# Routing interleaved with the output projection by token tile, expert weights loaded in pieces

## The chip, the core and the metric

The kernel runs on one core of a Trainium2 chip. TensorE (PE) multiplies matrices, VectorE (DVE) and ScalarE (ACT) do elementwise work and read PSUM, GpSimd (POOL) does elementwise work and issues the indirect transfers, SyncE (SP) issues most DMAs, and 16 DMA engines move the data. The metric is the device time of one execution in microseconds (us).

## The reference

Two layers (`DEPTH = 2`) over 512 tokens (`SEQ`) of width 1024 in float32, then a final RMSNorm:

```
for l in range(DEPTH):
    h = rms_norm(x, attn_norm_g[l]);  proj = h @ w_in[l]
    ya = banded_attention(...) @ w_branch_a[l]      # 8 heads, sinks
    yb = dilated_attention(...) @ w_branch_b[l]     # 3 groups of 4 heads
    merged = sigmoid(gate_a) * ya + sigmoid(gate_b) * yb
    x = x + merged @ w_out[l]                       # output projection
    x = x + hier_moe(rms_norm(x, ffn_norm_g[l]), ...)
```

`hier_moe` computes 4 group logits and 32 expert logits for each token, takes the best group, the best two experts inside it, and adds the two experts' SwiGLU outputs (1024 to 2 x 256 to 1024), weighted.

## The kernel before

A token tile is 128 tokens; there are four (`TT`), t = 0 to 3. Each layer goes through these stages.

- Projections, attention and gates, to about 372 us in the first layer. Weight tiles of 512 KB are streamed through a ring of two buffers (`raw`) by SP (`load_tile`); ACT rounds a tile to `w_hi` (`split_hi`, line 779), DVE computes the rest `w_lo` (`split_lo`, line 980), and TensorE makes three products (`three`, lines 431 to 433: hi*hi, lo*hi, hi*lo). `w_hi`/`w_lo` also have two buffers. SP may load tile i when tile i-2 has been split. Two semaphores carry this: `hi_ok`, `lo_ok` (a tile is split), and `w_used` (TensorE has used it).
- Output projection: eight weight tiles, called here out tiles 0 to 7. The loop `for dh in range(2)` goes over the two halves of the output columns, inside it `for kp in range(4)` over the weight tiles, and inside that over the four token tiles. Columns 0 to 511 of token tile t gather in bank t, columns 512 to 1023 in bank 4+t. DVE adds the banks to `x` (`xo_ok`). While this goes on, SP loads the weights of expert pair 0 and then of pair 1 in pieces of 512 KB (`load_piece`), between the `raw` tiles, all in one queue.
- Routing, after the last out tile: squares of `x` on ACT, `rstd` on DVE, transposes of `x` on TensorE (line 647) and copies into `xtr`, router logits (line 615), a second transpose, the normalised rows `xn2` (`h2_tile`) stored to DRAM by POOL (`h2_rows`, line 1392), and then on DVE a long chain of small instructions from the logits (line 1173) to the assignment `asg` (line 1212). TensorE adds up the assignments (`bank[6]`), DVE turns them into ranks (`rankm`), selections (`sel`, `choose`) and, with a matmul (`read_info`, line 669), into row indices (`slots`: `idx_h`, `idx_y`). `keep_busy` (line 447) are matmuls whose result nobody reads.
- Experts: 16 pairs. For pair n: POOL gathers its rows (`gather`, line 1397), TensorE turns them (`rows_in`, line 675), `up` (line 681) multiplies with the weights `gu`, then SiLU, `turn_z`, and `down` (line 694) with `dn`; POOL scatters the rows. The weights are 4 MB (`gu`) and 2 MB (`dn`) a pair in a ring of three buffers (`RING`). Pair 2's weights lie on the merged activations and may be loaded only when the output projection has ended (`w_used`); pair p's may be loaded when pair p-3 is done with its buffer (`gu_ok`, `dn_ok`).
- At the layer's end SP loads the scattered rows (`yld`) and DVE adds them to `x`.

Of the kernel before, what the change touches and what calls it, by code (L numbers as in the profile page):

```python
# [9 lines left out]
I32 = mybir.dt.int32  # L10
# [22 lines left out]
MORE_AT = {s: sum(1 for n in range(2, PAIRS) if n % RING == s) for s in range(RING)}  # L33
# [56 lines left out]
K_ORDER = [6, 7, 0, 1, 2, 3, 4, 5]  # L90

# [7 lines left out]
def hybrid_encoder(nc, x_in, stream, gu_w, dn_w, params, g_rows, consts, masks, out):  # L99
# [27 lines left out]
    info = at("info", o, [TT, 2, NE], F32R); o = after(o + 4 * TT * 2 * NE)  # L127
    idx_y = at("idx_y", o, [PAIRS], I32); o = after(o + 4 * PAIRS)
    idx_h = at("idx_h", o, [PAIRS], I32); o = after(o + 4 * PAIRS)
    small = at("small", o, [288], FP32); o = after(o + 4 * 288)  # L130
    gl8 = small[:, 96:128].rearrange("p (t n) -> p t n", n=8)
    cum = small[:, 128:288].rearrange("p (t n) -> p t n", n=NE)
# [30 lines left out]
    w_hi = [at(f"w_hi{i}", R_S + (8 + 8 * i) * KB, [1024], F32R) for i in range(2)]  # L163
    w_lo = [at(f"w_lo{i}", R_S + (12 + 8 * i) * KB, [1024], F32R) for i in range(2)]
    xtr = at("xtr", R_S + 8 * KB, [KD, T], FP32)
# [4 lines left out]
    xn2 = [at(f"xn2_{t}", R_H + 48 * KB + 4 * KB * t, [D], FP32) for t in range(2)] + [at("xn2_2", R_S, [D], FP32)]  # L170
# [4 lines left out]
    junk = at("junk", R_S + 4 * KB, [2, D], BF16)  # L175
    sel = at("sel", R_S + 4 * KB, [2, TT, P], F32R)

    rt = at("rt", R_S + 16 * KB, [2048], FP32)
# [20 lines left out]
    rankm = word(TT * NE, TT, NE)  # L199
    wts = word(TT * 8, TT, 8)  # L200
    elog = word(TT * NE, TT, NE)
    lgt = word(T)
    lsc = word(TT * NLOG, TT, NLOG)
    top_g = word(TT * 8, TT, 8)
    idx_g = word(TT * 8, TT, 8)
    top_e = word(TT * 8, TT, 8)
    idx_e = word(TT * 8, TT, 8)
    idxf = word(TT * 3, TT, 3)
    oh_g = word(TT * NGRP, TT, NGRP)
    el8 = word(TT * 8, TT, 8)  # L210
    oh1 = word(TT * NE, TT, NGRP, EPG)
    oh2 = word(TT * NE, TT, NGRP, EPG)
    elm = oh1
    oh8 = word(TT * 2 * EPG, TT, 2, EPG)
    asg = word(TT * NE, TT, NE)
    rtmp = elog
    ge = word(TT * NGRP, TT, NGRP)
    assert _w[0] <= 2048, _w[0]
# [9 lines left out]
    spare = small[:, 64:65]  # L228

    ctx = ExitStack()  # L230
    with ctx:
# [31 lines left out]
        h2_ok, h2_st0, h2_st = sems("h2_ok", "h2_st0", "h2_st")  # L263
# [58 lines left out]
        def _(sp):  # L322
# [46 lines left out]
            with sp.Fori(0, L) as l:  # L369
# [17 lines left out]
                for p in range(2, PAIRS):  # L387
                    if p >= RING:
                        sp.wait_ge(gu_ok, l * PAIRS + p - RING + 1)
                    load_gu(l, p)  # L390
                    if p >= RING:
                        sp.wait_ge(dn_ok, l * PAIRS + p - RING + 1)
# [1135 lines left out]
```

## Time and profile before

| | us |
|---|---|
| three runs | 1416.78, 1419.51, 1419.99 (median 1419.51) |
| the profiled execution's own time | 1414.65 |
| its span | 1413.0 |
| TensorE busy | 1241.5 (88%) |
| VectorE busy | 592.0 (42%) |
| ScalarE busy | 398.2 (28%) |
| GpSimd busy | 240.0 (17%) |
| mean granted TensorE clock | 0.955 of full speed |

The span is the time from the first to the last instruction in the profile. A busy TensorE is not one at its peak. Each time in the rows below is counted from the span's start; a releaser in square brackets names what the engine had waited for before the row.

### The profile page before, as it was taken

The page shows a single profiled execution, that of the slowest core. Times are in us where ns is not written, and L with a number is a line of the kernel's source. Part 1 is how long each engine was busy: PE and PEld are TensorE (multiplying, and loading weights), DVE is VectorE, ACT ScalarE, POOL GpSimd, SP SyncE. Part 2 cuts the span into 40 slices and gives each one's busy share as a digit, 9 for nine tenths or more (in the row PEclk, how much of TensorE's full clock was granted, in tenths as well). Part 3 has the DMA queues.
Part 4 walks back from the last instruction along what each step waited for, and adds up shares of the span by engine and source line. Part 5 has one row for each costly group of instructions (what it writes and reads, how often), then busy time and mean ns, then how long its engine had stood idle before and what let it go on. Part 6 is the DMA issues. An engine that isn't in the chain of part 4 may idle for free.

```text
span 1413.0 us, 18694 instructions
## 1 busy us (share of the span) xinstructions
PE 1241.5 (88%) x6416; PEld 813.5 (58%) x6417; DVE 592.0 (42%) x1395; ACT 398.2 (28%) x731; POOL 240.0 (17%) x183
## 2 busy tenths in 40 slices
PE   5999988999997998887489999889999979978881
PEld 5877766788884433332177777667888734423330
DVE  4467676233344222221254677753333432322115
ACT  5334335333231110000153444444332300100003
POOL 0314140022101111111003233201220011111100
PEclk9999999999999999998899999999999989999996
DMA  5432220463544899999433222106437539999975
GB/s 185 127 96 84 76 90 2 149 218 108 205 183 186 367 424 424 424 424 417 162 122 116 90 91 90 45 16 223 164 104 283 217 123 424 423 423 425 424 333 199
DMA packets 59486, 306.76 MB, mean 217 GB/s; under 512 B 11376, under 2 KB 11376, under 8 KB 45056
## 3 DMA queue, kind: packets, MB, share of 16 engines
q1 hardware_dynamic: 48256, 281.57, 51.3%
q0 software_dynamic: 10992, 23.25, 4.4%
q8 instruction: 50, 0.82, 0.2%
q10 hardware_dynamic: 144, 0.76, 0.1%
q14 instruction: 44, 0.36, 0.1%
HBM read 290.33 MB, written 23.07 MB: 222 GB/s over the span
## 4 chain that ended last, share of the span: by engine, by line
PE 61%; DMA 21%; DVE 7%; issue 4%; ACT 3%; DVEq 3%; SPq 0%; ACTq 0%; POOL 0%; POOLq 0%
DMA gu<-in_gu_w 17%; PE bank L431 13%; PE bank L433 13%; PE bank L432 13%; PE bank L681 10%; PE bank L694 4%; PE bank L566 2%; DVEq L1062 1%; DMA h_rows<-xn 1%; ACT prob L850 1%; PE bank L502 1%; DVE prob L1085 1%; PE bank L675 1%; PE bank L533 1%; DMA yld<-y_rows 1%
## 5 line engine op out<-in xcount | busy, mean ns | idle before, releaser
L681 PE MATMUL bank<-gu,xgt 128*64 128x512 f32 x1024 | 245.9, 636 | 49.8 <-DMA gu<-in_gu_w 46.8
L431 PE MATMUL bank<-h_hi,w_hi 128*128 128x512 f32 x640 | 253.4, 396 | 6.1 <-DVE h_lo L1022 3.6
L433 PE MATMUL bank<-h_hi,w_lo 128*128 128x512 f32 x640 | 249.5, 390 | 0.0
L432 PE MATMUL bank<-h_lo,w_hi 128*128 128x512 f32 x640 | 249.1, 389 | 0.0
L980 DVE TENSOR_TENSOR w_lo<-raw,w_hi 128x1024 fp32r<-128x1024 f32 x112 | 139.2, 1243 | 185.2 <-ACT w_hi L779 184.3
L681 PEld LDWEIGHTS bank<-gu,xgt 128*64 128x64 f32 x1024 | 79.1, 146 | 213.1 <-issue 168.5
L779 ACT ACTIVATE w_hi<-raw 128x1024 fp32r<-128x1024 f32 x112 | 118.1, 1055 | 101.2 <-PE bank L433 101.2
L431 PEld LDWEIGHTS bank<-h_hi,w_hi 128*128 128x128 f32 x640 | 120.2, 188 | 32.4 <-DVE h_lo L1022 4.0
L433 PEld LDWEIGHTS bank<-h_hi,w_lo 128*128 128x128 f32 x640 | 120.1, 188 | 25.5
L432 PEld LDWEIGHTS bank<-h_lo,w_hi 128*128 128x128 f32 x640 | 120.3, 188 | 23.7
L694 PE MATMUL bank<-dn,zt 128*64 128x512 f32 x512 | 116.9, 598 | 6.2 <-ACT zt L939 3.3
L1294 DVE TENSOR_TENSOR z<-bank,sil 128x256 f32<-128x256 f32 x32 | 13.6, 425 | 248.2 <-ACT sil L937 248.2
L1369 POOL TENSOR_TENSOR swp<-swp,cst 128x512 f32<-128x512 f32 x34 | 48.7, 1431 | 289.2 <-DMA swp<-pj 289.2
L937 ACT ACTIVATE sil<-bank 128x256 f32<-128x256 f32 x32 | 12.3, 384 | 293.7 <-PE bank L681 293.7
L1397 POOL DMA_INDIRECT xg<-h_rows,idx_h x32 | 32.4, 1012 | 350.8 <-DVE idx_y L1254 337.3
L850 ACT ACTIVATE prob<-prob,small 128x256 f32<-128x256 f32 (+2 forms) x96 | 64.7, 675 | 58.4 <-DVE small L1067 58.4
L1384 POOL TENSOR_TENSOR mab<-mab 128x512 f32<-128x512 f32 x16 | 35.2, 2199 | 263.8 <-DVE mab L1135 263.8
L1085 DVE TENSOR_SCALAR prob<-prob,small 128x256 f32<-128x256 f32 (+2 forms) x96 | 73.5, 807 | 5.1 <-issue 1.7
L694 PEld LDWEIGHTS bank<-dn,zt 128*64 128x64 f32 x512 | 34.0, 136 | 64.6 <-issue 55.3
L1268 DVE COPY yb<-bank 128x512 f32<-128x512 f32 x32 | 22.1, 692 | 110.4 <-PE bank L694 63.1
L933 ACT ACTIVATE yb<-bank 128x512 f32<-128x512 f32 x32 | 19.1, 597 | 134.5 <-PE bank L694 76.2
L1033 DVE TENSOR_TENSOR rca<-pj,cst 128x512 f32<-128x512 f32 x34 | 29.7, 872 | 50.1 <-ACT pj L837 50.1
(181 smaller groups left out, 1627.2 us busy)
## 6 DMA issues: line engine op xcount, KB each, us to landing
gu<-in_gu_w SPq DMA_DIRECT2D x28, 4096.0 KB, 37.6
raw<-in_stream SPq DMA_DIRECT2D x112, 512.0 KB, 3.4
dn<-in_dn_w SPq DMA_DIRECT2D x28, 2048.0 KB, 36.6
gu<-in_gu_w SPq DMA_DIRECT2D x32, 512.0 KB, 5.5
swp<-pj SPq DMA_DIRECT2D x136, 64.0 KB, 2.0
dn<-in_dn_w SPq DMA_DIRECT2D x16, 512.0 KB, 5.7
yld<-y_rows SPq DMA_DIRECT2D x16, 512.0 KB, 7.1
h_rows<-xn POOLq DMA_DIRECT2D x8, 512.0 KB, 10.5
```

What stands on the lines that cost most here:

```text
L431: mm(dst, ah, bh, start=start, stop=False)
L432: mm(dst, ah, bl, start=False, stop=False)
L433: return mm(dst, al, bh, start=False, stop=stop)
L681: last = mm(bank[b][e * CAP:(e + 1) * CAP, :], xgt[:, x_s, k, e * CAP:(e + 1) * CAP], gu[w_s][:, e, k, :], start=k == 0, stop=k == KD - 1)
L694: last = mm(bank[4 + half][e * CAP:(e + 1) * CAP, :], zt[:, f, e * CAP:(e + 1) * CAP], dn[w_s][:, e, f, half * T:(half + 1) * T], start=f ...
L779: run(w_hi[i % 2][:, :], raw[:, i % 2, :], ACT.Copy).then_inc(hi_ok, 1)
L850: last = run(p, p, ACT.Exp, bias=nmx[:, 2 * s + h:2 * s + h + 1], scale=-1.0, accum_out=rsum[:, 2 * s + h:2 * s + h + 1])
L980: tt(w_lo[i % 2][:, :], raw[:, i % 2, :], w_hi[i % 2][:, :].bitcast(FP32), ALU.subtract).then_inc(lo_ok, 1)
L1085: last = ts(p, p, den[:, 2 * s + h:2 * s + h + 1], None, ALU.mult)
L1369: g.tensor_tensor(swp[:, r % 2, :], swp[:, r % 2, :], c(C_SIN, T), ALU.mult).then_inc(sn_ok, 1)
L1384: g.tensor_tensor(mab[:, half, 0, :], mab[:, half, 0, :], mab[:, half, 1, :], ALU.add).then_inc(sum_ok, 1)
L1397: pool.indirect_dma_start(out=xg[n % 2][:, :], out_offset=None, in_=h2_rows[:, :], in_offset=bass.IndirectOffsetOnAxis(ap=idx_h[:, n:n + 1 ...
```

## The change

It has four parts. (1) The second half of the output projection goes over token tiles outside and weight tiles inside; between them stand the transposes of `x` (`turn_x`) and the router logits, each in half tiles (`HALVES`). The logits are computed with the tokens on the partitions, so the second transpose goes. For this all four weight tiles of the second half must be held at once: `OUT_SLOT` gives them two more buffers. (2) The routing on DVE is done in two groups of two token tiles (`choose_group`, `rank_group`): the first inside the projection, the second after it. `h2_tile` and the transposes' copies are on ACT; the count of rounds and the weights `wts` come after the first three `slots`. (3) The weights of pairs 2, 3, 13, 14 and 15 are loaded in pieces (`PARTS`), `dn` in two, and `up_pair` waits for each piece. (4) Pair 2's `gu` is split around the first two gathers: SP waits for them before its last two pieces; pair 3's first piece waits for the first half of pair 0's `up` (`gu_half`).

```diff
+PARTS = {2: 4, 3: 2, PAIRS - 3: 2, PAIRS - 2: 4, PAIRS - 1: 4}
...
+OUT_SLOT = [0, 1, 0, 1, 2, 3, 0, 1]
+HALVES = [(0, 0), (1, 0), (0, 1), (1, 1), (2, 0), (3, 0), (2, 1), (3, 1)]
...
+    W_AT = (R_S + 8 * KB, R_S + 16 * KB, R_Q + 32 * KB, R_Q + 40 * KB)
...
                 sp.wait_ge(w_used, (l + 1) * NT)
-                for p in range(2, PAIRS):
-                    if p >= RING:
-                        sp.wait_ge(gu_ok, l * PAIRS + p - RING + 1)
-                    load_gu(l, p)
...
+                load_dn_part(l, 2, 0)
+                load_dn_part(l, 2, 1)
+                load_gu_part(l, 2, 0)
+                load_gu_part(l, 2, 1)
+                for s in range(2):
+                    sp.wait_ge(xg_ld[s], (l * (PAIRS // 2) + 1) * 16)
+                load_gu_part(l, 2, 2)
+                load_gu_part(l, 2, 3)
+                sp.wait_ge(gu_half, l + 1)
+                load_gu_part(l, 3, 0)
+                sp.wait_ge(gu_ok, l * PAIRS + 1)
+                load_gu_part(l, 3, 1)
...
+                BETWEEN = {(0, 3): [("x", 0), ("x", 1)], (1, 3): [("l", 0), ("l", 1), ("x", 2), ("x", 3)],
+                           (2, 1): [("l", 2), ("l", 3), ("x", 4), ("x", 5)], (2, 3): [("l", 4), ("l", 5)],
+                           (3, 1): [("x", 6)], (3, 3): [("l", 6), ("x", 7), ("l", 7)]}
+                for t in range(TT):
                     for kp in range(4):
...
+                        if t == 0:
+                            need(pe, lo_ok, l * NT + NQ + NGATE + 4 + kp + 1)
+                        last = out_step(1, kp, t)
...
+                        for what, n in BETWEEN.get((t, kp), []):
+                            if what == "x":
+                                turn_x(n)
+                            else:
+                                router_logits(n)
+                        if (t, kp) == (3, 1):
...
+                            pe.wait_ge(rk_ok, 2 * l + 1)
+                            count(bank[5][:, 0:2 * NE], asg[:, 0:2, :], True, True, False)
...
+                keep_busy(bank[7][:, :], 4)
+                pe.wait_ge(rk_ok, 2 * l + 2)
...
+                    for k in range(KD):
+                        if k % 4 == 0:
+                            pe.wait_ge(xtd_ok, 2 * (n0 + n) + 1 + k // 4)
+                        if n in PARTS and k % w == 0:
+                            pe.wait_ge(gu_part[n][k // w], (l + 1) * 16)
+                        last = up_step(n % 2, n % 2, n % RING, k)
+                        if n == 0 and k == KD // 2 - 1:
+                            last.then_inc(gu_half, 1)
...
+            def split_out_hi(l, n):
+
+                i, s = NQ + NGATE + n, OUT_SLOT[n]
+                act.wait_ge(raw_ld[i % 2], (l * (NT // 2) + i // 2 + 1) * 16)
+                if s < 2:
+                    act.wait_ge(w_used, l * NT + NQ + NGATE + max(m for m in range(n) if OUT_SLOT[m] == s) + 1)
+                else:
+                    need(act, mlo_ok, l * KD + KD + 1)
+                run(w_hi[s][:, :], raw[:, i % 2, :], ACT.Copy).then_inc(hi_ok, 1)
...
+                dve.wait_ge(w_used, l * NT + NQ + NGATE + 4)
+                add_out(0, 0)
+                add_out(0, 1)
+                split_out_lo(l, NOUT - 1)
...
+                rank_group(0)
+                choose(0, 0, None, (0, 1))
+                dve.wait_ge(w_used, l * NT + NT)
+                add_out(1, 3)
+                norm_tile(3)
...
+                scale_tile(3)
...
+                choose_group(1)
+                rank_group(1)
+                choose(0, 0, sel_ok, (2, 3))
```

TensorE's program at the start of the projection's second half, before: one weight tile (`w_hi_90` with `w_lo_92`) for all token tiles, and the next `lo_ok` wait only 24 matmuls later.

```order
L431 MATMUL bank<-w_hi_90,m_hi 128x512 [waits lo_ok]
L432 MATMUL bank<-w_lo_92,m_hi 128x512
L433 MATMUL bank<-w_hi_90,m_lo 128x512
L431 MATMUL bank<-w_hi_90,m_hi 128x512
L432 MATMUL bank<-w_lo_92,m_hi 128x512
L433 MATMUL bank<-w_hi_90,m_lo 128x512
```

TensorE's program at the same place in the changed kernel: the first token tile's last two weight tiles (out tiles 6 and 7, in the buffers `w_hi_90` and `w_hi_91`), then the first transposes.

```order
L463 MATMUL bank<-w_hi_90,m_hi 128x512 [waits lo_ok]
L464 MATMUL bank<-w_lo_94,m_hi 128x512
L465 MATMUL bank<-w_hi_90,m_lo 128x512
L463 MATMUL bank<-w_hi_90,m_hi 128x512
L464 MATMUL bank<-w_lo_94,m_hi 128x512
L465 MATMUL bank<-w_hi_90,m_lo 128x512
L292 REGISTER_ALU
L463 MATMUL bank<-w_hi_91,m_hi 128x512 [waits lo_ok]
...
L671 MATMUL bank<-cst,x 128x128 [waits xo_ok]
L671 MATMUL bank<-cst,x 128x128 x3
```

A weight tile now has 6 matmuls between two `lo_ok` waits where it had 24, for the first token tile; the other token tiles have no such wait.

SP's program behind the last `raw` load, before: pair 2 whole, then pair 3 on `gu_ok` and `dn_ok`.

```order
L338 ISA [waits w_used]
L338 DMA gu_62<-in_gu_w 128x2x4096
L343 ISA
L343 DMA dn_65<-in_dn_w 128x2x2048
L338 ISA [waits gu_ok]
L338 DMA gu_60<-in_gu_w 128x2x4096
```

The same place in the changed kernel:

```order
L354 ISA [waits w_used]
L354 DMA dn_65<-in_dn_w 128x2x1024
L354 ISA
L354 DMA dn_65<-in_dn_w 128x2x1024
...
L349 ISA [waits xg_ld1,xg_ld0]
L349 DMA gu_62<-in_gu_w 128x2x1024
L349 ISA
L349 DMA gu_62<-in_gu_w 128x2x1024
L349 ISA [waits gu_half]
L349 DMA gu_60<-in_gu_w 128x2x2048
L349 ISA [waits gu_ok]
L349 DMA gu_60<-in_gu_w 128x2x2048
```

Half of pair 2's `gu` has moved behind the landing of the gathers of pairs 0 and 1 (`xg_ld`), and pair 3's first piece stands on `gu_half`.

## Rows read from the trace of the kernel before

**Rows 1.** The page: chain that ended last; two groups (busy, mean ns | idle before).

```profile
PE 61%; DMA 21%; DVE 7%; issue 4%; ACT 3%; DVEq 3%; SPq 0%; ACTq 0%; POOL 0%; POOLq 0%
...
L980 DVE TENSOR_TENSOR w_lo<-raw,w_hi 128x1024 fp32r<-128x1024 f32 x112 | 139.2, 1243 | 185.2 <-ACT w_hi L779 184.3
...
L779 ACT ACTIVATE w_hi<-raw 128x1024 fp32r<-128x1024 f32 x112 | 118.1, 1055 | 101.2 <-PE bank L433 101.2
```

**Rows 2.** Timeline of SP's DMA issues: start us, us, queue, line, what, count.

```profile
386.04 0.33 SPq L334 DMA_DIRECT2D raw<-in_stream  x1
...
391.45 5.77 SPq L334 DMA_DIRECT2D raw<-in_stream  x2
416.26 0.39 SPq L338 DMA_DIRECT2D gu<-in_gu_w  x1
...
462.32 0.37 SPq L338 DMA_DIRECT2D gu<-in_gu_w  x1
...
474.77 0.37 SPq L338 DMA_DIRECT2D gu<-in_gu_w  x1
```

**Rows 3.** The windows view, us of each stretch: PE, PEld, DVE, ACT, POOL, PEclk, DMA share, GB/s.

```profile
377.00:395.00 18.00, 18.00 (x81) 14.93 (x80) 3.68 (x3) 3.92 (x5) 1.30 (x1) 1.00 1.01 394
480.00:536.00 56.00, 55.48 (x282) 21.73 (x278) 15.77 (x53) 6.05 (x13) 8.56 (x9) 1.00 1.01 423
663.00:664.00 1.00, 1.00 (x4) 0.24 (x2) 0.00 (x0) 0.00 (x0) 0.00 (x0) 0.50 1.02 434
680.00:682.00 2.00, 2.00 (x13) 0.72 (x10) 0.00 (x0) 0.00 (x0) 0.00 (x0) 1.00 0.10 39
...
697.00:705.00 8.00, 0.00 (x0) 0.00 (x0) 4.67 (x5) 1.35 (x3) 0.59 (x1) 0.50 0.97 373
```

**Rows 4.** Timeline of TensorE: the first `up`, and the layer's last pairs.

```profile
455.05 7.09 PE L681 MATMUL bank<-gu,xgt 128*64 128x512 f32 x32 [1.46 <-DVE xgt L1261]
...
661.56 8.78 PE L681 MATMUL bank<-gu,xgt 128*64 128x512 f32 x32 [2.58 <-DMA gu<-in_gu_w]
...
677.25 7.09 PE L681 MATMUL bank<-gu,xgt 128*64 128x512 f32 x32 [1.40 <-DMA gu<-in_gu_w]
...
686.18 3.65 PE L694 MATMUL bank<-dn,zt 128*64 128x512 f32 x16 [0.47 <-ACT zt L939]
```

**Rows 5.** Timeline of POOL: the last store, the first two gathers.

```profile
432.86 0.53 POOL L1392 DMA_DIRECT2D h_rows<-xn  x1 [5.72 <-DVE xn L1005]
446.28 1.06 POOL L1397 DMA_INDIRECT xg<-h_rows,idx_h  x1 [12.89 <-DVE idx_y L1254]
447.64 1.02 POOL L1397 DMA_INDIRECT xg<-h_rows,idx_h  x1 [0.30 <-issue]
```

**Rows 6.** Timeline of DVE: first and last instruction from logits to assignment.

```profile
432.21 0.30 DVE L1173 TENSOR_TENSOR rt<-bank,small 128x144 f32<-128x144 f32 x1
...
438.09 0.29 DVE L1212 TENSOR_TENSOR rt<-rt 128x128 f32<-128x128 f32 x1
```

**Rows 7.** Lines by form, TensorE, 400 to 462 us: count | busy us, mean ns | idle.

```profile
L615 PE MATMUL bank<-xtr,par 128*36 128x128 f32 x64 | 7.6, 274 | 1.0 <-DVE xtr L1146 1.0
...
L647 PE MATMUL bank<-cst,x 128*128 128x128 f32 x32 | 4.1, 276 | 0.0
```

**Rows 8.** One line's view, L334: landing of the `raw` load issued at 386.0.

```profile
DMA to landing us min/median/max: 7.3/7.3/7.3
```

**Rows 9.** The same view: landing of the `raw` load issued at 391.4.

```profile
DMA to landing us min/median/max: 6.9/6.9/6.9
```

**Rows 10.** The view of L1397, 446 to 449 us: landing of the two gathers.

```profile
DMA to landing us min/median/max: 3.5/3.9/4.3
```

**Rows 11.** The view of L1392, 421 to 434 us: landing of the four stores.

```profile
DMA to landing us min/median/max: 6.1/10.5/11.7
```

**Rows 12.** Timeline of SP's DMA issues in the second layer.

```profile
1110.20 0.39 SPq L338 DMA_DIRECT2D gu<-in_gu_w  x1
...
1157.87 0.37 SPq L338 DMA_DIRECT2D gu<-in_gu_w  x1
```

More of the change, by code:

```diff
@@ L32 @@
 RING = 3
[L33 removed]
+PARTS = {2: 4, 3: 2, PAIRS - 3: 2, PAIRS - 2: 4, PAIRS - 1: 4}
+WHOLE = [n for n in range(2, PAIRS) if n not in PARTS]
+MORE_AT = {s: sum(1 for n in WHOLE if n % RING == s) for s in range(RING)}
 PARAMS = KD * NLOG + NLOG + 2 * KD + 8
@@ L662, in _, with out_step @@
-                mm(bank[6][:, 0:TT * NE], c(C_TRI, P), asg[:, :, :], start=False, stop=True).then_inc(lgd_ok, 1)
-                keep_busy(bank[7][:, :], 2)
-                def read_info(s, e0, done):
+                def out_step(dh, kp, t, l=l):
+                    i = NQ + NGATE + dh * 4 + kp
+                    for kk in range(2):
+                        k = 2 * kp + kk
+                        tok = slice(t * P, (t + 1) * P)
+                        last = three(bank[4 * dh + t][:, :], (m_hi[:, k, tok], m_lo[:, k, tok]),
+                                     wt(i, kk, 512, OUT_SLOT[dh * 4 + kp]), k == 0, k == KD - 1)
+                    return last
@@ new lines, in router_logits @@
+                def router_logits(n, l=l):
+                    t, half = HALVES[n]
+                    pe.wait_ge(xtra_ok, l * NH + n + 1)
+                    if n == NH - 1:
+                        pe.wait_ge(xtrd_ok, l + 1)
+                    if n == 0:
+                        pe.wait_ge(xo_ok, l * 2 * TT + TT)
+                    if n == 4:
+                        pe.wait_ge(xo_ok, l * 2 * TT + TT + 1)
+                    for j in range(4):
+                        last = mm(bank[3 + t // 2][:, (t % 2) * NLOG:(t % 2 + 1) * NLOG], xtr[:, n % 2, j, :], wr[:, 4 * half + j, :],
+                                  start=n % 4 == 0 and j == 0, stop=n % 4 == 3 and j == 3)
+                    last.then_inc(lg_ok, 1)
@@ L688, in turn_z, with down_step @@
                     last.then_inc(done, 1)
+                def down_step(w_s, half, f):
+                    for e in range(2):
+                        last = mm(bank[4 + half][e * CAP:(e + 1) * CAP, :], zt[:, f, e * CAP:(e + 1) * CAP],
+                                  dn[w_s][:, e, f, half * T:(half + 1) * T], start=f == 0, stop=f == 1)
+                    return last
                 def down(w_s, done):
@@ L704, in landed @@
                     else:
-                        nth = sum(1 for p in range(2, n) if p % RING == n % RING)
+                        nth = sum(1 for p in WHOLE if p < n and p % RING == n % RING)
                         pe.wait_ge(later[n % RING], (l * MORE_AT[n % RING] + nth + 1) * 16)
@@ L725, in down_pair @@
                         pe.wait_ge(yd_ok, n0 + n)
-                    down(n % RING, dn_ok)
-                pe.wait_ge(route_ok, l + 1)
+                    if n in PARTS:
+                        for f in range(2):
+                            pe.wait_ge(dn_part[n][f], (l + 1) * 16)
+                            for half in range(2):
+                                last = down_step(n % RING, half, f)
+                        last.then_inc(dn_ok, 1)
+                    else:
+                        landed(first_dn, dn_ld, n)
+                        down(n % RING, dn_ok)
                 where(0)
```

504 lines of the change are left out of this document (274 added, 230 removed).

## The prediction, made before the changed kernel ran

> **What bounds the kernel now.** I read the page's chain first. TensorE holds 61% of it and DMA 21% [rows 1], and these are two stages. Up to the end of the output projection TensorE is busy without a break; in the expert stage the DMA engines are. The windows view shows the second: from 480 to 536 us a DMA share of 1.01 at 423 GB/s, while pair 3 and what follows is loaded [rows 3]. The timeline of SP shows where that stream begins. Pair 2 is issued at 416.3, when the projection ends, and nothing more until 462.3, when pair 0's `up` has released its buffer [rows 2]. Between them lie the routing, the gathers and the first `up`, and the DMA engines have little to do. From 462.3 the stream is full to the last pair, so a layer ends at a fixed time after its start: pair 15's `gu` is there at 677.25, 215 us later [rows 4]. Thirteen pairs of 6.29 MB take 193 us at 423 GB/s, and the gathers and scatters share the queues for the rest. So the change has two places to gain: start this stream earlier, and shorten what follows its last byte.
>
> I write E for the end of the output projection, 416.0 in the first layer (pair 2 is issued right behind it [rows 2]).
>
> **The projection's second half.** It starts at E - 4 x 5.44 = 394.2, as an out tile takes 5.4 us (the two reloads are 5.41 apart [rows 2]).
> Moved into it are 28 of 32 transposes and 24 of 32 router steps. The transposes took 4.1 us for 32, so 3.6; the router's 64 matmuls took 7.6 us [rows 7]. Theirs are a new form (128 weights, 36 columns instead of 36 and 128): below, the 36 columns could save half, above, nothing is faster than now. The transposes, with 128 weights each, go at 0.13 us, which is the nearest row, so I take 0.13 x 48 = 6.2. The first group's counting is 6 calls of two matmuls, at 0.13 us 1.6. Together 11.4 us, to 427.4.
>
> **The stall.** In the first token tile each weight tile is needed 1.36 us after the one before, where it was 5.44. Are they there? Out tile 5 is issued at 386.04 and lands 7.3 us later, at 393.3 [rows 2, 8]: with 1.06 and 1.24 us of splitting [rows 1] it is ready at 395.8, needed at 395.5. Out tile 6 was issued at 391.45 and landed 6.9 us later, 398.3 [rows 9]. It is behind twelve 512 KB pieces of pair 1 in one queue, and from 377 to 395 that queue is full (share 1.01 [rows 3]). Its issue waits for the split of out tile 4, which the new buffers let happen only 0.8 us earlier, and behind a full queue this gains nothing: landed about 398.0, ready at 400.6, but needed at 397.1. That is a wait of 3.5 us. Out tile 7's `w_lo` stands on DVE behind out tile 6's and two additions to `x` of 0.65: 403.1 against 402.1, another 1.1. The second half's first token tile so ends 5.0 us late. A gap of 2.58 us before an `up` made it take 8.78 us, where 1.40 left it at 7.09 [rows 4], and the granted clock behind it is 0.50, which is 1.2 of 2.4 GHz [rows 3]. I charge the gap the same 1.6. Bounds of this item: 0 (if the tile comes in time) and 5.0 + 3.2. So E = 427.4 + 5.0 + 1.6 = 434.0, 18 us later than now. I expect no further wait in it: ACT and DVE have 5.4 us for each token tile, and the first group's assignment (3.9 us, below) has 7.9 us of TensorE work to hide under before the counting asks for it.
>
> **From E to the gathers.** Left behind E are router steps 6 and 7 with one transpose and its copies, 3.6 us; the second group; ranks; selection; `slots`. The chain from logits to `asg` took 432.21 to 438.09 and 0.29 more for four tiles, 6.2 us [rows 6]. It is the same number of dependent steps with half the work; at half of it it would be 3.1, at no saving 6.2. I take 3.9, since some ten dependent steps of 0.25 remain. Then counting and ranks 1.2, selection 0.5, reading and `slots` 1.1, POOL's issue 1.0 (estimates from the same 0.25 us a dependent step and 1.06 an issue [rows 5]). The sum is 3.6 + 3.9 + 1.2 + 0.5 + 1.1 + 1.0 = 11.3: gather 0 at E + 11.3 = 445.3, where it is now at 446.28 [rows 5]. 18 us of projection are paid, 19 us of routing are saved, and the gather stands nearly where it stood. Before, the last store was issued at 432.86, held up by the first one's landing; stores took 6.1 to 11.7 us [rows 5, 11] beside pair 2's load. Now it is issued at E + 5 and has 6 us; it shares with packets a quarter as long. If it lands later, up to E + 13, the cost is 2 us a layer.
> The second gather follows 1.36 us behind and lands in 3.5 [rows 5, 10]. SP issues pair 2's last two pieces at E + 16.5 = 450.5.
>
> **From there to the stream.** Before, the stream needed the turn, the first copy and a whole `up` (7.09 us [rows 4]) after the gathers. Now pieces of pair 2 fill this time: 2.1 MB, 4.95 us at 423 GB/s. Pair 3's first piece is released by half an `up`, about E + 21.4, before that runs out at E + 24; then `gu_ok` at E + 25, and pair 4 one TensorE pair later (12.4 us, from 462.3 to 474.8 [rows 2]), just ahead of the stream. So it is continuous, and the start that compares with 462.3 is 450.5 + 4.95 = 455.5: 6.8 us gained. This is covered by TensorE at full clock; if pair 0's `up` runs at half, up to 4 us of gap come back.
>
> **Smaller pieces.** The pieces of pairs 2, 14 and 15, and the `dn` of 3 and 13, move 4 KB rows instead of 16 and 8. The nearest row with 4 KB rows in a full queue is the 394 GB/s against 423 [rows 3]. The 18.9 MB after the gathers then take 48.0 instead of 44.7 us: I charge 3.0 (0 to 3.3).
> A rule speaks against the pieces: the Trainium skill (DMA: Bandwidth & Descriptors, § Bandwidth) measured 341 GB/s for a DMA of 1 MB and 425 for one of 16 MB. By it the 18.9 MB would cost 10.7 us instead of 3.0. The trace disagrees so far: there 0.5 MB pieces behind each other in a full queue ran at 394.
>
> **The layer's end.** Pair 15's last piece lands at 677.25, and six of eight steps of `up` are done by then: 1.8 us are left of 7.09, so 5.3 are saved. `down` would start 1.84 behind, at 680.9. DMA is still at 0.10 until 682 [rows 3], which is the last `dn` on one or two engines; its first half is there, its second at about 683, so it ends at 684.6 instead of 689.8: 5.2 saved. What follows, scatter and `yld`, is as before. Pair 14's gap and half clock go too, but that is hidden by the stream.
>
> **The sum.** First layer: -6.8 + 3.0 - 5.2 = -9.0. Second layer: its projection ends 693.9 us after the first's, its pair 3 is issued at 1157.87 [rows 12], 1.6 us later than that distance would put it, and the changed one has no reason to be: -10.6. Together -19.6 us on the execution's own 1414.65: 1395. The median of the runs is 4.9 above that execution, so I predict 1419.5 - 19.6 = 1400 us.
>
> **Rivals.** No change that can be measured is within 0.2%, 2.8 us.
> 1. The weights come in time. For: out tile 6's issue depends on splits that are now earlier; a queue that drains a little faster suffices. Against: it was behind the pieces before as well. Then -6.6 more in each layer: about 1387.
> 2. The stream has a gap. Pair 0's `up` runs at half clock behind the routing's waits, as pair 14's partly did (8.78 us for 7.09 [rows 4]; wholly at half it is 14), and `keep_busy` ahead of it is one call shorter. Or the last store lands late. +4 to 6 a layer: about 1410. Against: before, that `up` took 7.09.
> 3. Pieces are slow: each has its own start and end on every engine, and engines idle between them. The slowest row with 4 KB rows is the load of `yld`, 373 GB/s [rows 3]; 18.9 MB at that take 50.7 us, 3 more than I charge: about 1406, and with twice that loss 1412. The full share of 1.01 beside 394 speaks against. By the Trainium skill's 341 GB/s (the page and section above) it would be 1415.
> 4. Slower: TensorE loses its clock in the projection. It now has six places where it waits for ACT or DVE copies. If they were late by 2 us each, the clock would fall again and again and the 33 us of the second half go at 0.50. All of it at half is +33 a layer; it decides where 20 of the 33 us are at half or waiting, which costs the 10 us that a layer gains; at 16 us a layer the result is about 1432. Against: between two such places lie 2.7 to 5.4 us of dense matmuls, and the copies are 0.6 us.
> 5. The change does not do what it says: the stream's start is not earlier and only the tail counts: -2 a layer, 1415.
>
> **The numbers.** My forecast 0.60 (1393 to 1406), rival 1 0.13, rival 2 0.10, rival 3 0.07, rival 4 0.05, rival 5 0.05. The range of 8 in 10 takes rival 1 and most of rivals 2 and 3: 1385 to 1412. Slower by over 0.2%: rival 4 and a little of the others, 0.06; within 0.2%: 0.04; faster 0.90.
>
> **What the profile after would show.** Right: TensorE idle 3 to 4 us before the third weight tile of the first token tile, and the clock at 0.50 behind it; pair 2 issued 17 to 19 us later than 416.3; gather 0 at 444 to 447; pair 2's last pieces issued at about 450.5; DMA full from there; `up` of pair 15 ending 2 us after its last piece. Wrong: no idle time at out tile 6 (rival 1); a DMA share well under 1 between 455 and 475 (rival 2); below 390 GB/s in pairs 14 and 15 (rival 3); idle time before `turn_x`, the router steps or the counting (rival 4).

## The result and the profile after

The changed kernel took 1398.99 us, the median of 4 runs (1398.0 to 1403.66), against 1419.75 us before (4 runs, 1416.78 to 1420.4) on the same chip. The medians are 20.8 us apart. The ratio of the two kernels' runs is 0.9866, with a 95% interval of 0.9845 to 0.9886: by it the change is worth 16 to 22 us. The profiled execution took 1399.06 us. The lines that answer to [rows 1], from its page (its span, the shares of the chain, and the group of the projection's matmuls that now waits):

```profile
span 1397.4 us, 18940 instructions
...
PE 60%; DMA 15%; SPq 7%; DVE 7%; issue 4%; ACT 3%; DVEq 2%; ACTq 0%; POOL 0%; POOLq 0%
...
L463 PE MATMUL bank<-w_hi,m_hi 128*128 128x512 f32 x128 | 52.4, 409 | 8.2 <-DVE w_lo L1129 8.1
```

DMA fell from 21% of the chain to 15%; SPq, SP's own issuing, rose from 0% to 7% (its lines are those of the pieces, L349 and L354), so the two together stand where DMA stood. The projection has 8.2 us of idle time that it did not have: two layers of the stall that was predicted. It stands in the timeline of TensorE (start, duration, instruction, idle time before it and its releaser) as 3.48 and 0.56 us in the first layer. The third and fourth rows are pair 0's transposes and its `up`, the next two the end of pair 15, and the last is the same stall in the second layer:

```profile
399.87 0.50 PE L463 MATMUL bank<-w_hi,m_hi 128*128 128x512 f32 x1 [3.48 <-DVE w_lo L1129]
...
402.20 0.79 PE L463 MATMUL bank<-w_hi,m_hi 128*128 128x512 f32 x1 [0.56 <-DVE w_lo L1129]
...
450.75 1.09 PE L737 MATMUL bank<-cst,xg 128*128 128x128 f32 x8 [0.78 <-DMA xg<-h_rows,slot]
452.63 7.09 PE L742 MATMUL bank<-gu,xgt 128*64 128x512 f32 x32 [0.79 <-DVE xgt L1383]
...
675.24 1.94 PE L742 MATMUL bank<-gu,xgt 128*64 128x512 f32 x8 [1.83 <-DMA gu<-in_gu_w]
...
679.03 3.65 PE L758 MATMUL bank<-dn,zt 128*64 128x512 f32 x16 [0.47 <-ACT zt L1065]
...
1089.00 0.50 PE L463 MATMUL bank<-w_hi,m_hi 128*128 128x512 f32 x1 [3.44 <-DVE w_lo L1129]
```

The windows view of TensorE (busy time, granted clock, DMA share, GB/s) shows the clock behind the stall at 0.50, which is 1.2 of 2.4 GHz, and then the DMA engines around the gathers:

```profile
399.00:402.00 3.00, 1.78 (x6) 0.87 0.00 0
402.00:408.00 6.00, 5.80 (x18) 0.50 0.00 1
440.00:445.00 5.00, 3.65 (x23) 0.72 1.01 413
445.00:450.00 5.00, 4.97 (x9) 0.60 0.73 266
450.00:455.00 5.00, 3.46 (x20) 1.00 0.52 165
455.00:480.00 25.00, 24.66 (x126) 1.00 1.02 413
```

Against [rows 2] stands SP's timeline: pair 2 is issued at 432.95 instead of 416.26, pair 4 at 472.36 instead of 474.77, and between them four pieces of pair 2 and two of pair 3:

```profile
432.95 0.95 SPq L354 DMA_DIRECT2D dn<-in_dn_w  x2
434.09 26.17 SPq L349 DMA_DIRECT2D gu<-in_gu_w  x6
465.48 0.93 SPq L354 DMA_DIRECT2D dn<-in_dn_w  x2
472.36 0.37 SPq L339 DMA_DIRECT2D gu<-in_gu_w  x1
```

Against [rows 5, 6] stand GpSimd's timeline (the last store of rows, the first gather), VectorE's (the first `slots`), and the view of that one store with its time to landing:

```profile
437.45 0.53 POOL L1540 DMA_DIRECT2D h_rows<-xn  x1 [7.87 <-ACT xn L1026]
446.50 1.05 POOL L1545 DMA_INDIRECT xg<-h_rows,slot  x1 [8.52 <-DVE slot L1376]
```
```profile
442.50 0.32 DVE L1376 TENSOR_SCALAR slot<-bank 64x2 int32<-64x2 f32 x2
```
```profile
L1540 POOL DMA_DIRECT2D h_rows<-xn x1: 531/531/531, 437.4 to 437.4; - x1
...
DMA to landing us min/median/max: 8.0/8.0/8.0
```

The row of the gather names `slot` as its releaser, but `slot` was there at 442.8. What came last is the store, 437.45 + 8.0 = 445.4. In e1, e3, e6, e9 and e10 below, the first gather likewise stands 1.0 to 1.1 us behind the landing of that store. A releaser that had long been done is the sign of another wait.

**The layer cut in four.** To compare kernels I cut each profiled execution at the start of out tile 3's `w_lo` (A; 384.56 before, 383.64 after), the first issue of pair 2 (E), the start of pair 0's `up` (U) and the first issue of `yld` (Y). From Y to the second layer's A no kernel here differs in its code. All values are differences of such starts, in us.

| | A to E | E to U | U to Y | A to Y, second layer | both A to Y | Y to A, same code |
|---|---|---|---|---|---|---|
| before | 31.7 | 38.8 | 240.5 | 308.8 | 619.8 | 382.9 |
| after | 49.3 | 19.7 | 234.9 | 298.4 | 602.3 | 385.2 |
| e1 pieces late | 42.2 | 19.9 | 235.0 | 295.9 | 593.0 | 388.2 |
| e2 whole at end | 47.8 | 20.0 | 237.9 | 302.6 | 608.3 | 384.0 |
| e3 no split | 47.5 | 23.9 | 239.9 | 307.4 | 618.7 | 385.1 |
| e4 old routing | 31.7 | 37.6 | 235.2 | 301.1 | 605.6 | 388.4 |
| e5 gap filled | 48.2 | 19.3 | 235.1 | 299.2 | 601.8 | 383.5 |
| e6 store first | 47.8 | 22.9 | 236.7 | 304.1 | 611.5 | 385.7 |
| e7 = e1 + e6 | 43.0 | 23.3 | 237.8 | 298.6 | 602.7 | 387.7 |
| e8 piece per gather | 43.1 | 19.7 | 235.3 | 297.2 | 595.2 | 387.6 |
| e9 routing alone | 47.6 | 22.5 | 242.1 | 311.5 | 623.8 | 383.7 |
| e10 = e9 + late | 43.0 | 23.2 | 241.4 | 306.5 | 614.0 | 385.6 |
| e11 old, less filling | 31.7 | 35.5 | 234.6 | 299.6 | 601.4 | 387.0 |

The last column warns: the same instructions took between 382.9 and 388.4 us. A single profile's end is no measure for less than 5 us; the stretches are better, but they are not exact either. Before E the changed kernel, e2, e3, e6 and e9 have the same program, and their ten values of A to E (two layers each) go from 46.6 to 49.3, with seven of them between 47.3 and 47.8. The changed kernel's 49.3 is the longest of the ten, its 46.6 in the second layer the shortest.

### The profile page after: what moved, and what is told of

The parts are those of the page before. It is cut to its first block, busy times and chain, and to the rows that moved or that the text cites. A ratio compares the mean times of both kernels' runs of the same rounds, so it can differ in the third digit from the quotient of the medians.

```text
span 1397.4 us, 18940 instructions
## 1 busy us (share of the span) xinstructions
PE 1231.0 (88%) x6424; PEld 809.6 (58%) x6425; DVE 586.8 (42%) x1353; ACT 412.2 (29%) x761; POOL 239.1 (17%) x183
## 4 chain that ended last, share of the span: by engine, by line
PE 60%; DMA 15%; SPq 7%; DVE 7%; issue 4%; ACT 3%; DVEq 2%; ACTq 0%; POOL 0%; POOLq 0%
PE bank L463 13%; PE bank L465 12%; PE bank L464 12%; PE bank L742 9%; DMA gu<-in_gu_w 9%; SPq L349 4%; PE bank L758 4%; SPq L354 3%; DMA raw<-in_stream 2%; PE bank L598 2%; DVEq L1186 2%; PE bank L737 1%; ACT prob L949 1%; PE bank L534 1%; DVE prob L1209 1%
## 5 line engine op out<-in xcount | busy, mean ns | idle before, releaser
L742 PE MATMUL bank<-gu,xgt 128*64 128x512 f32 x1024 | 242.4, 624 | 43.0 <-DMA gu<-in_gu_w 41.1
L742 PEld LDWEIGHTS bank<-gu,xgt 128*64 128x64 f32 x1024 | 75.6, 143 | 205.7 <-issue 188.7
L1104 DVE TENSOR_TENSOR w_lo<-raw,w_hi 128x1024 fp32r<-128x1024 f32 x102 | 128.0, 1255 | 149.6 <-ACT w_hi L868 148.6
L868 ACT ACTIVATE w_hi<-raw 128x1024 fp32r<-128x1024 f32 x102 | 107.5, 1054 | 57.3 <-PE bank L465 57.3
L1441 DVE TENSOR_TENSOR z<-bank,sil 128x256 f32<-128x256 f32 x32 | 13.6, 425 | 234.6 <-ACT sil L1063 234.6
L1517 POOL TENSOR_TENSOR swp<-swp,cst 128x512 f32<-128x512 f32 x34 | 47.5, 1396 | 291.1 <-DMA swp<-pj 291.1
L1063 ACT ACTIVATE sil<-bank 128x256 f32<-128x256 f32 x32 | 12.3, 384 | 270.0 <-PE bank L742 270.0
L1545 POOL DMA_INDIRECT xg<-h_rows,slot x32 | 32.4, 1012 | 331.5 <-DVE slot L1376 323.0
L463 PE MATMUL bank<-w_hi,m_hi 128*128 128x512 f32 x128 | 52.4, 409 | 8.2 <-DVE w_lo L1129 8.1
```

The source lines that it names most:

```text
L463: mm(dst, ah, bh, start=start, stop=False)
L742: last = mm(bank[b][e * CAP:(e + 1) * CAP, :], xgt[:, x_s, k, e * CAP:(e + 1) * CAP], gu[w_s][:, e, k, :], start=k == 0, stop=k == KD - 1)
L868: run(w_hi[i % 2][:, :], raw[:, i % 2, :], ACT.Copy).then_inc(hi_ok, 1)
L1104: tt(w_lo[i % 2][:, :], raw[:, i % 2, :], w_hi[i % 2][:, :].bitcast(FP32), ALU.subtract).then_inc(lo_ok, 1)
L1517: g.tensor_tensor(swp[:, r % 2, :], swp[:, r % 2, :], c(C_SIN, T), ALU.mult).then_inc(sn_ok, 1)
```

## The experiments

All ran in five rounds beside the kernel before. Theory A is the prediction's account, with the two sizes that the profile after gave: a stall of 4.0 us with 3 us lost to the clock, and the late store. Times are compared with the changed kernel's 1399.0. It ran in another round than they did, so where two times are close the ratios to the kernel before are given too.

**e1: pair 1's last pieces later.** Is out tile 6 late because of the queue or because of its splits?

```diff
-                    if NQ + NGATE + 2 <= i < NQ + NGATE + 6:
-                        for n in range(3):
-                            load_piece(l, 1, 3 * (i - NQ - NGATE - 2) + n)
+                    for n in {2: range(3), 3: range(3, 6), 7: range(6, 12)}.get(i - NQ - NGATE, ()):
+                        load_piece(l, 1, n)
```

> Pair 1's twelve pieces are issued three behind out tile 2's load, three behind out tile 3's and six only behind out tile 7's, so none of them stands between the loads of out tiles 5, 6 and 7. Theory A (the second half waits because out tile 6's load is queued behind pieces, and the wait of 3.48 us then costs TensorE its clock): the two waits of 3.48 and 0.56 us for w_lo go, the granted clock stays above 0.9 through the projection, and each layer gains the 4.0 us of waiting and the 3.0 us that 6 us at 0.50 cost; about 1399 - 14 = 1385 us. Rival 1 (the tile is late because of its splits on ACT and DVE, not because of the queue): the wait stays at over 2.5 us and the time within 3 us of the changed kernel. Rival 2 (the time is given back later: the last six pieces delay the last store of rows, pair 2's pieces and so the gathers): the wait goes, but the first gather moves by less than 4 us, about 1392.

1391.9 us (1388.0 to 1392.4, ratio 0.9797, interval 0.9776 to 0.9818), 7 less than the changed kernel by the medians and 10 by the ratios. The windows view of its TensorE has full clock where the changed kernel had 0.50:

```profile
399.00:408.00 9.00, 9.00 (x57) 1.00 0.57 228
435.00:440.00 5.00, 4.25 (x11) 0.50 0.94 387
440.00:445.00 5.00, 3.29 (x12) 0.88 0.39 112
```

A to E fell by 7.1, as theory A said, and 6.8 of it came through to Y. That settles the queue as the cause of the stall. In the second layer a wait of 1.20 us was left and the changed kernel had kept its clock there (below), so only 2.5 were gained: 9.3 in the two stretches, not 14. The profiled executions are 6.7 apart, since the unchanged code took 3.0 longer in this one. The number of theory A was wrong because it gave both layers the first one's clock. Nor is 7.1 the usual price of the stall: against the seven values of 47.3 to 47.8 it is 5.1 to 5.6.

**e5: the gap filled.** Does the emptiness of the wait cost the clock?

```diff
+                        if (t, kp) == (0, 2):
+                            keep_busy(bank[7][:, :], 7)
```

> The changed kernel with seven matmuls of keep_busy on bank 7 (nobody reads them) ahead of the wait for out tile 6's low part, so that TensorE has something to do in the 3.48 us it waits. Theory A (the wait itself is set by the load, and only its emptiness costs the clock): the third weight tile is still used at 399 to 401 us, the granted clock stays at 1.00 from 401 to 408 instead of 0.50 to 0.61, and the projection ends 3 us earlier in the first layer; in the second, where the changed kernel's clock stayed at 1.00 after the same wait, nothing: about 1399 - 3 = 1396 us. Rival (the clock falls for another reason, such as the dense matmuls behind the wait): clock and time unchanged, 1399.

1397.4 us (ratio 0.985, interval 0.9828 to 0.9873), not told apart from 1399.0. The timeline of TensorE shows why so little, and the windows what the clock did:

```profile
395.15 6.17 PE L479 MATMUL bank<-cst 128*128 128x512 f32 x14
400.76 0.79 PE L463 MATMUL bank<-w_hi,m_hi 128*128 128x512 f32 x1
```
```profile
395.00:401.00 6.00, 6.00 (x17) 1.00 0.22 80
402.00:404.00 2.00, 2.00 (x11) 1.00 0.00 0
404.00:408.00 4.00, 4.00 (x23) 1.00 0.02 6
```

The clock stayed at 1.00, in the second layer too. One layer alone would prove little, since the changed kernel kept its clock once behind the unfilled wait. But the five kernels with this wait unfilled (the changed one, e2, e3, e6, e9) show 0.50 behind it, or from its last part on, in nine layers of ten. With the filling it was kept in two of two, and the dense matmuls behind the wait are the same. That speaks for the filling as what kept the clock; it is not proof.

It paid for nothing all the same. On VectorE's timeline `w_lo` was ready at 397.44 + 1.23 = 398.7, and the 14 matmuls took 0.44 us each at full clock, 6.2 us for a wait of 3.5: they held TensorE to 400.8. A to E is 48.2 in both layers, 1.1 less than the changed kernel's first layer, but no less than the 47.3 to 47.8 of most unfilled ones. Half as much filling would have ended in time; it wasn't tried.

**e3: no split.** Is it the two pieces behind the gathers, and pair 3's early one, that bring the gain?

```diff
-                for s in range(2):
-                    sp.wait_ge(xg_ld[s], (l * (PAIRS // 2) + 1) * 16)
                 load_gu_part(l, 2, 2)
                 load_gu_part(l, 2, 3)
-                sp.wait_ge(gu_half, l + 1)
-                load_gu_part(l, 3, 0)
                 sp.wait_ge(gu_ok, l * PAIRS + 1)
+                load_gu_part(l, 3, 0)
                 load_gu_part(l, 3, 1)
```

> All of pair 2's pieces are issued at the end of the projection, with no wait for the gathers between them, and both pieces of pair 3 only when pair 0's up is done. Theory A: pair 2's last two pieces then share the queue with the last store of rows and the two gathers, and nothing is left to fill the time of the first up: the stream starts 4.95 us of transfer later, and the gathers land later too; each layer is longer by 3 us (if store and gathers get their share of the queue) to 8 us (if the store lands only when the 6.3 MB are through): 1405 to 1415. Rival (what fills the time around the gathers doesn't matter, since the stream is bound later anyway): within 3 us of the changed kernel.

1417.1 us (ratio 0.9984, interval 0.9969 to 0.9998): 18 more by the medians, 17 by the ratios, 16.4 in the stretches. This one edit gives back nearly the whole gain. Its windows, beside those of the changed kernel above, the view of its first two gathers, and the landing of its last store (issued at 436.60):

```profile
445.00:450.00 5.00, 4.64 (x6) 0.56 1.03 416
450.00:455.00 5.00, 1.72 (x8) 0.78 0.63 247
455.00:460.00 5.00, 4.22 (x12) 0.53 0.19 54
460.00:465.00 5.00, 5.00 (x25) 1.00 0.00 0
465.00:480.00 15.00, 14.66 (x80) 1.00 0.92 355
```
```profile
L1542 POOL DMA_INDIRECT xg<-h_rows,slot x2: 1022/1038/1054, 445.6 to 447.0; - x2
...
DMA to landing us min/median/max: 7.2/7.4/7.6
```
```profile
L1537 POOL DMA_DIRECT2D h_rows<-xn x1: 531/531/531, 436.6 to 436.6; - x1
...
DMA to landing us min/median/max: 8.0/8.0/8.0
```

The gathers were issued 0.9 us earlier than in the changed kernel (445.65) but landed in 7.2 to 7.6 us instead of 3.6 to 4.2, behind pair 2's rest; the first `up` began 3.4 us later and ran in part at half clock; and then the DMA engines had nothing until pair 3. From 450 to 480 they were idle for 1.85 + 4.05 + 5.0 + 1.2 = 12.1 us. The changed kernel's are idle for 1.35 + 2.4 = 3.75 us between 445 and 455. That is 8.4 apart, of the 9.2 by which E to Y is longer (263.8 against 254.6).

The other kernels bear this out. I added up the idle time of the DMA engines in slices of 2.5 us over the 65 us behind E, first layer, for the seven kernels that have the new routing and pieces at both ends: 5.1 in the changed kernel, 5.3 in e1, 4.8 in e5, 4.4 in e8, 8.9 in e6, 10.3 in e7 and 13.9 in e3. E to Y less this idle time is 249.5 to 250.8 in all seven, while E to Y itself goes from 254.4 to 263.8.

**e2: pairs 13 to 15 whole.** `PARTS` is `{2: 4, 3: 2}`.

> Pairs 13, 14 and 15 are loaded whole again, with 16 and 8 KB rows; pairs 2 and 3 stay in pieces. Theory A (the pieces at the end save 5.2 us behind the last byte of a layer and cost up to 2.5 us, since 4 KB rows move slower): 2 to 4 us a layer longer, about 1399 + 5 = 1404. Rival (rows of 4 KB cost nothing in a full queue: the share is 1.01 to 1.05 with either): 5 us a layer longer, 1409. Rival (pieces are slow, and by as much as they save): no change, 1399.

1404.5 us (ratio 0.9907, interval 0.9885 to 0.9929): 5.6 more, 6.0 in the stretches, theory A's number. The interval just touches the changed kernel's 0.9845 to 0.9886, so the size is uncertain by some 3 us. From the start of the last weights' `up` to Y it took 17.5 us (670.37 to 687.82), where the changed kernel took 12.3 from its last piece (675.24 to 687.55): 5.1 to be had. 2 of them go to slower rows, since Y came only 3.0 later measured from pair 4's issue. The windows view of TensorE has the rows' price: first the changed kernel with pieces, then this one with whole tiles.

```profile
640.00:650.00 10.00, 8.54 (x42) 1.00 1.02 398
650.00:660.00 10.00, 7.19 (x32) 1.00 1.03 412
```
```profile
640.00:650.00 10.00, 9.53 (x44) 0.88 1.01 423
650.00:660.00 10.00, 7.77 (x30) 0.83 1.00 423
```

**e4: the old routing with the pieces.** The kernel before, with parts 3 and 4 alone.

> The kernel before, its projection and routing untouched, with the change's parts 3 and 4 alone: expert weights in pieces at both ends and pair 2's weights split around the first gathers. Theory A (the routing between the token tiles moves work without shortening the way to the gather, 18 us paid against 19 saved, and the gain comes from filling the queue around the gathers and from the layer's end): gather 0 at 443 to 445 us, since the last store no longer has all of pair 2 beside it, and the time about that of the changed kernel, 1393 to 1402. Rival (the routing in the projection brings half of the gain or more): 1406 to 1412. Rival (parts 3 and 4 bring nothing by themselves): 1417 to 1420.

1403.8 us (1399.8 to 1404.9, ratio 0.9883, interval 0.9861 to 0.9905). Parts 3 and 4 alone bring 15 to 16 us by the medians. The changed kernel is 4.8 faster by the medians, 2.4 by the ratios and 3.3 in the stretches, and the two intervals overlap: the difference is not clear of the noise. The gather went out at 441.87, a little better than expected, and A to U was 69.3 us against the changed kernel's 69.0: the whole routing between the token tiles, with its stall, had moved the first `up` by 0.3 us.

**e11: the same with less filling.** In e4 the gathers had landed by 447.8, but the transposes waited for `keep_busy` (timeline of TensorE, then the edit):

```profile
443.34 6.07 PE L483 MATMUL bank<-cst 128*128 128x512 f32 x8
449.24 1.04 PE L711 MATMUL bank<-cst,xg 128*128 128x128 f32 x8
451.75 4.51 PE L716 MATMUL bank<-gu,xgt 128*64 128x512 f32 x20 [1.47 <-DVE xgt L1325]
```
```diff
-                keep_busy(bank[6][:, :], 4)
+                keep_busy(bank[6][:, :], 2)
```

> The old routing with the pieces (1403.8), with two calls of keep_busy instead of four ahead of pair 0's transposes. There the eight filling matmuls ran at half clock from 443.34 to 449.24 us, while both gathers had landed by 447.8: the transposes waited for a filling. Theory A (old and new routing bring the gathers equally early, and what is left between the two kernels is this filling): the transposes start at about 446.5, the first up 2.5 us earlier in each layer, and the time is 1398 to 1400, that of the changed kernel, so the routing between the tiles with its wait at out tile 6 is worth nothing. Rival (the shorter filling lets the clock drop during the first up, which then takes 9 us or more, or the stream is bound by something else): 1402 to 1406.

1403.2 us (1399.7 to 1404.4, ratio 0.9891, interval 0.9873 to 0.991): the time shows no gain. In the stretches E to U is 2.1 shorter and both A to Y are 4.2 shorter, a little less than 2.5 a layer. The two disagree, and I leave the worth of this edit open. What the stretches do show is the way to the first `up`: A to U is 67.2 us here against 69.0 in the changed kernel and 62.1 in e1. Measured against an old routing with this filling, the new one lengthened that way by 1.8 us with its stall, and shortens it by 5.1 without.

**e9 and e10: the routing alone, without and with the late pieces.** `PARTS` is empty and SP loads pairs 2 to 15 as before; e10 has e1's edit besides.

> The changed kernel's projection and routing (parts 1 and 2) with the weights of all pairs from 2 on loaded whole, in the order of the kernel before: gu and dn of pair 2 at the end of the projection, pair 3 when pair 0's up is done. Theory A (the routing between the tiles costs about as much as it saves, and it moves pair 2's load to where the last store and the gathers need the queue): the store lands 10 us or more after its issue, the first up starts at 456 us or later, and the time is that of the kernel without the split, 1417, plus 2 to 5 us for the layer's end: 1418 to 1424, no faster than the kernel before or slower. Rival (the routing brings 5 us by itself, the difference between the changed kernel and the old routing with the pieces): 1412 to 1416.

> The same, with pair 1's last six pieces behind out tile 7's load. Theory A (the wait at out tile 6 is worth 7 us a layer in the first layer and 3 to 7 in the second, wherever the rest of the time goes): 7 to 12 us less than the same kernel with the pieces early. Rival (without the split the store and the gathers wait for the queue, and an earlier end of the projection is hidden): under 4 us less.

e9 took 1422.0 us (12 runs, 1417.7 to 1425.5, ratio 1.0016, interval 1.0006 to 1.0027), e10 1409.7 (ratio 0.9921, interval 0.9904 to 0.9938). Parts 1 and 2 alone bring nothing; they are, if anything, 2 to 3 us slower. With most of the stall taken away they bring 9 by the medians, 11 by the ratio. e9's timelines of GpSimd show what its pair 2, whole and first in the queue, does to the store and the gather (its landing took 10.4 us):

```profile
434.53 0.53 POOL L1519 DMA_DIRECT2D h_rows<-xn  x1 [7.85 <-ACT xn L1005]
445.98 1.05 POOL L1524 DMA_INDIRECT xg<-h_rows,slot  x1 [10.92 <-issue]
```

The gain of e10 over e9, 12.4 us, is larger than that of e1 over the changed kernel, though its stall is the same; by the stretches it is 9.8 against 9.3.

**e6, e7: the last store before pair 2's `gu`.** Can the late store be had earlier?

```diff
                 load_dn_part(l, 2, 1)
+                for s in range(2):
+                    sp.wait_ge(h2_st[s], (l + 1) * 2 * 16)
                 load_gu_part(l, 2, 0)
```

> The changed kernel, but SP waits for the last store of normalised rows to land before it issues the first two pieces of pair 2's gu; the two pieces of dn still go at the end of the projection. Theory A (the first gather waits for that store, 446.50 where its indices were there at 442.8, and the store takes 8.0 us only because it shares the queue with pair 2's 4.2 MB): the store lands in 4 to 5 us, gather 0 is issued at 443 to 444, and each layer is 2 to 2.5 us shorter if the two pieces still fill the queue until the gathers have landed: about 1395. Rival (the pieces issued later only move the same bytes to behind the gathers, so the stream is as long as before): within 2 us, 1397 to 1401, or up to 3 us a layer slower.

> Both edits: pair 1's last six pieces behind out tile 7's load (which by itself gave 1391.9), and SP's wait for the last store ahead of pair 2's gu. If the two costs are independent, each layer gains what the two gave apart: 1391.9 minus what the store's edit gives on the changed kernel, 1387 to 1389 by theory A; with the rival, 1390 to 1394.

e6 took 1408.2 us (ratio 0.9923, interval 0.9906 to 0.9941), 9 more; e7 1400.8 (ratio 0.9869, interval 0.9847 to 0.9891), 9 more than e1. Theory A fell here, and the rival's 3 us a layer were too few. The view of the last store, then the windows, then that of the gathers:

```profile
L1542 POOL DMA_DIRECT2D h_rows<-xn x1: 531/531/531, 436.8 to 436.8; - x1
...
DMA to landing us min/median/max: 7.2/7.2/7.2
```
```profile
440.00:445.00 5.00, 3.58 (x22) 0.79 0.35 141
445.00:450.00 5.00, 4.86 (x6) 0.53 0.94 328
450.00:455.00 5.00, 1.64 (x8) 0.81 0.57 201
```
```profile
L1547 POOL DMA_INDIRECT xg<-h_rows,slot x2: 1021/1037/1053, 445.1 to 446.4; - x2
...
DMA to landing us min/median/max: 7.1/7.3/7.6
```

With 2.1 MB ahead of it instead of 4.2 the store landed only 0.8 us sooner than in the changed kernel, and no sooner than in e5, where it took 7.2 behind the 4.2 MB. While SP waited for it, the DMA engines were idle for 3.2 us between 440 and 445; and the pieces released then met the gathers, which landed in 7.1 to 7.6 us. So what stands ahead of the gathers must be through when they go out. In the changed kernel's order it nearly is: its first two gathers landed in 3.6 to 4.5 us, counting both layers.

**e8: a piece for each gather.** e1's kernel, with the wait for the second gather only ahead of pair 2's fourth piece.

> The kernel with pair 1's pieces late, and pair 2's third piece released when the first gather has landed, the fourth when the second has, instead of both behind both. In the profile of the late pieces the DMA share is 0.39 from 440 to 445 us, while SP waits for the two gathers. Theory A (each idle us of the queue between the projection's end and pair 3 is paid at the layer's end): the third piece is issued about 1.4 us earlier, the gap is that much shorter, but the second gather then shares the queue: 0 to 1.4 us a layer less, about 1390. Rival (the second gather is slowed by more than is gained, and pair 0 starts later): 1392 to 1396.

1386.7 us (1382.4 to 1393.7, ratio 0.9764, interval 0.9743 to 0.9785). The interval overlaps that of e1, and the profile shows no effect: both pieces were issued within 0.7 us in either kernel (444.2 and 444.8, e1 444.0 and 444.5), since the two gathers land within 0.7 us of each other, and the stretches are 595.2 against 593.0. Its profiled execution was the slowest of its five. Whether it beats e1 stays open; both beat the changed kernel and the kernel before.

## Why the prediction was right, and by how much its steps were off

The forecast was 1400 (1385 to 1412), the result 1399.0. Its mechanism is what the runs showed. That the number came within 1 us is luck: terms cancelled, and the two layers' clocks fell one better and one worse than was usual.

- **The projection's second half.** +18 in the sum, +17.6 in the profile (49.3 against 31.7). The stall was put at 5.0 and was 4.04, at out tiles 6 and 7 as named. The lost clock was put at 1.6 us and cost 3.0, since 6 us were at 0.50. In the second layer the same stall of 3.44 and 0.67 us was followed by a clock of 1.00, so A to E grew by 14.9 only. In most layers of e2, e3, e6 and e9, with the same program up to E, it grew by 15.7 to 16.1, with a clock lost for about half as long: there 1.6 was the right charge. What was too high is the moved work: put at 11.4, it came to about 10.1 (e1's 42.2 - 31.7, less its wait of 0.4).
- **From E to the gather.** 11.3 in the sum, 13.55 in the profile (446.50 - 432.95). The chain was right: the second group took 436.03 to 440.07, so 4.0 for 3.9, and `slots` was there 9.9 after E. The step that failed is "now it is issued at E + 5 and has 6 us": the store was issued at E + 4.5 and took 8.0. The 2 us that were named for this case were paid in both layers: the gather was 2.2 us later than forecast in the first, and 1.8 in the second (1132.47 - 1119.37 = 13.1). Rival 2 had a part of the truth.
- **From there to the stream.** Pieces filled the time as worked out. The continuous stream was to begin at 450.5 and began at 451.64, with a share of 0.52 before 455. One sum in the prediction is wrong: two pieces issued at E + 16.5 that take 4.95 us run out at E + 21.5, not at E + 24, so pair 3's first piece at E + 21.4 had no time to spare. It had none in the run either: it was issued at 456.47, 4.8 us behind 451.64, just as the two ran out. From E to Y the layer lost 24.7 us where 27 were predicted.
- **Smaller pieces.** 3.0 charged a layer. The last three pairs alone cost 5.1 - 3.0 = 2.1 in the first layer of e2; what pair 2 adds wasn't measured apart. The Trainium skill (DMA: Bandwidth & Descriptors, § Bandwidth) has 341 GB/s for a transfer of 1 MB, measured with transfers issued from GpSimd. These pieces, issued by SP one behind the other, moved at 398 to 412, so that figure did not hold for this queue.
- **The layer's end.** 5.2 predicted, 5.1 measured with e2.
- **The sum.** First layer -9.0 predicted, -7.1 in the stretches (303.9 against 311.0): A to E came out 0.4 better than forecast, E to Y 2.3 worse, and that is the late store. Second layer -10.6 predicted, -10.4 measured: there the clock was kept and the moved work was less, which paid for the store. Together -19.6 predicted and -17.5 measured. The medians are 20.8 apart, the two profiled executions 15.6, since the unchanged code took 2.3 longer in the one after.
- **The rivals.** Rival 1 (weights in time) did not happen, but e1 made it happen by another queue order and gave 1391.9; the prediction had put it at 1387. Rival 3 is refuted by the rates above, rival 4 by the timeline (no wait before `turn_x`, the router steps or the counting above 0.8 us), rival 5 by e3.

What the prediction did not say, and the experiments do: the four parts are not worth their sum. Beside the new routing the split is worth 16 to 18 us (e3) and the pieces at the end about 6 (e2). The routing between the tiles adds 2 to 5 us to parts 3 and 4, not clear of the noise (e4), and nothing by itself (e9), but 9 by itself once most of the stall is gone (e10). It shortens A to U only by as much as the stall leaves: against e4, 0.3 us in the changed kernel and 7.3 in e1. So the prediction's "18 us of projection are paid, 19 us of routing are saved" was right, and it means that parts 1 and 2 as they stand hardly pay.

## What to carry to other kernels

Where one stage is bound by DMA and the one ahead of it isn't, count the idle time of the DMA engines between them: here nearly each idle us was a us of the layer (e3: 8.4 of 9.2, and e6 and e7 with it), and work moved to another engine only counts if it shortens that gap. Keep large loads out of the queue where a small transfer on the path is due: a weight tile behind pair 1's pieces cost 3 to 7 us a layer (e1, e10), a gather behind pair 2's rest 3.5. And a filling that keeps the clock must end before what it waits for, or it costs what it saves (e5; e4 by the stretches of e11).

## What the runs showed of the hardware that was not expected

A store of 512 KB landed in 2.9 to 3.9 us while the DMA engines had little else to do, in 7.2 with 2.1 MB of weights issued ahead of it (e6), in 7.2 to 8.1 with 4.2 MB (the changed kernel, e1, e2, e5), and in 10.4 with 6.3 MB issued as two whole transfers (e9). But with the same 6.3 MB issued as six pieces it landed in 8.0 (e3). So the amount ahead doesn't set it; whether the size of the transfers or that of their rows does was not tried apart.

The Trainium skill (DMA: Bandwidth & Descriptors, § Queues, rings and completion order) says that the write of a transfer's semaphore lands only after all earlier writes of that DMA engine, across its queues. That doesn't mean that all that was issued ahead must be through. e3's store had landed at 436.60 + 8.0 = 444.6, and from 445 to 450 the engines still moved 2.1 MB, while only two gathers of 0.5 MB each had been issued behind the store: at least 1 MB of pair 2, issued before it, was still to come. Whether that rule or plain sharing of the bandwidth delays the store, no run here separates.

The same gap of TensorE did not always cost its clock: behind 3.48 us in the first layer the granted clock was 0.50 for 6 us, behind 3.44 us in the second layer of the same execution it stayed at 1.00. In e3, e6 and e9, behind 3.42 to 3.47 us, it fell in all six layers. And code that nobody changed took 382.9 to 388.4 us between Y and A. A part of that is the clock: with the same 1948 matmuls TensorE was busy for 350.5 us in e5's stretch of 383.5, and for 356.0 us in e4's of 388.4, at mean granted clocks of 0.97 and 0.96. Why the clock differs there wasn't tried.
